# Seven products instead of eight for w_down, interleaved with w_up, in a one-core decoder layer

## What is computed

```
h = RMSNorm(x);  [b, c, xt, v] = h @ W_in
x = x + concat(short_conv(b, c, xt), pool_mix(v)) @ W_out
u = relu(RMSNorm(x) @ W_up)          # 2048 -> 8192
x = x + (u * u) @ W_down             # 8192 -> 2048
out = RMSNorm(x)
```

## Time and profile before

| | us |
|---|---|
| median of 3 runs | 1001.91 (1000.73 to 1002.18) |
| the profiled execution, device time | 1000.99 |
| its span in the trace | 999.2 |
| TensorE busy in it | 986.5 |
| VectorE busy | 586.4 |
| ScalarE busy | 419.6 |
| GpSimd busy | 1.4 |

### The profile page before, as it was taken

The page is one execution under the profiler, slowest core; times in us unless marked ns, Lnnn a source line. Parts: engine busy times, 40 slices in busy tenths (PEclk is TensorE's granted clock), DMA queues, the critical chain, the costliest instruction groups (busy, mean ns, idle before and its releaser), DMA issues.

```text
span 999.2 us, 12457 instructions
## 1 busy us (share of the span) xinstructions
PE 986.5 (99%) x5088; PEld 847.2 (85%) x5088; DVE 586.4 (59%) x428; ACT 419.6 (42%) x325; POOL 1.4 (0%) x9
## 2 busy tenths in 40 slices
PE   8999999999999999999999999999999999999996
PEld 7888888888888888888888888888888888888885
DVE  6597777655554766544656654556565445656453
ACT  6644435354443434333444433343433334444342
POOL 0000000000000000000000000000000000000000
PEclk9999999999999999999999999999999999999998
DMA  9956543555544655555455455545545554555512
GB/s 327 392 194 229 190 188 122 215 211 190 189 169 169 233 189 195 183 208 177 165 211 206 176 203 191 187 151 213 209 183 207 176 204 132 211 209 205 187 66 84
DMA packets 29694, 193.52 MB, mean 194 GB/s; under 512 B 3296, under 2 KB 3552, under 8 KB 7136
## 3 DMA queue, kind: packets, MB, share of 16 engines
q1 hardware_dynamic: 29232, 190.85, 52.1%
q10 hardware_dynamic: 288, 1.18, 0.3%
q0 software_dynamic: 144, 1.05, 0.3%
HBM read 190.97 MB, written 2.10 MB: 193 GB/s over the span
## 4 chain that ended last, share of the span: by engine, by line
PE 94%; DMA 3%; SPq 1%; DVE 1%; ACT 0%; issue 0%; ACTq 0%
PE ps L343 44%; PE ps L252 33%; PE ps L255 17%; DMA w_raw<-w_stream 3%; SPq L208 1%; PE ps L277 0%; PE ps L329 0%; SPq L193 0%; DVE w_lo L628 0%; ACT w_hi L449 0%; PE ps L317 0%; DVE val L635 0%; PE ps L276 0%; PE ps L279 0%; ACT cross L483 0%
## 5 line engine op out<-in xcount | busy, mean ns | idle before, releaser
L628 DVE TENSOR_TENSOR w_lo<-w_raw,w_hi 128x2048 fp32r<-128x2048 f32 x172 | 392.0, 2291 | 280.4 <-ACT w_hi L449 279.7
L449 ACT ACTIVATE w_hi<-w_raw 128x2048 fp32r<-128x2048 f32 x172 | 326.8, 1912 | 344.0 <-PE ps L343 210.8
L252 PE MATMUL ps<-act_a,w_hi 128*128 128x512 f32 x1472 | 351.1, 391 | 0.0
L343 PE MATMUL ps<-w_hi,act_b 128*128 128x512 f32 x1280 | 345.3, 390 | 0.0
L252 PEld LDWEIGHTS ps<-act_a,w_hi 128*128 128x128 f32 x1472 | 271.0, 188 | 52.5
L343 PEld LDWEIGHTS ps<-w_hi,act_b 128*128 128x128 f32 x1280 | 239.8, 188 | 49.3
L343 PE MATMUL ps<-w_lo,act_b 128*128 128x512 f32 x640 | 199.7, 389 | 0.0
L255 PEld LDWEIGHTS ps<-act_a,w_lo 128*128 128x128 f32 x1472 | 188.6, 191 | 7.0
L255 PE MATMUL ps<-act_a,w_lo 128*128 128x256 f32 x1472 | 191.1, 283 | 0.0
L343 PEld LDWEIGHTS ps<-w_lo,act_b 128*128 128x128 f32 x640 | 120.2, 188 | 25.0
L635 DVE TENSOR_TENSOR val<-ps,cross 128x1024 f32<-128x1024 f32 x26 | 31.8, 1223 | 47.2 <-ACT cross L455 47.2
(11 more groups left out here) (68 smaller groups left out, 164.3 us busy)
## 6 DMA issues: line engine op xcount, KB each, us to landing
w_raw<-w_stream SPq DMA_DIRECT2D x172, 1024.0 KB, 4.8
w_raw<-w_stream SPq DMA_DIRECT2D x16, 256.0 KB, 7.9
x<-x_rows SPq DMA_DIRECT2D x2, 1024.0 KB, 17.4
mix_mem<-x_t SPq DMA_DIRECT2D x3, 512.0 KB, 8.2
out<-x SPq DMA_DIRECT2D x6, 256.0 KB, 2.7
mix_mem<-pool_w ACTq DMA_DIRECT2D x1, 1024.0 KB, 9.1
mix_mem<-g_final POOLq DMA_DIRECT2D x1, 1024.0 KB, 5.0
out<-val SPq DMA_DIRECT2D x2, 256.0 KB, 2.1
```

Source lines behind the costliest of these rows:

```text
L252: return pe.matmul(ps[:, bank, :], weights_hi, act, start=first, stop=False)
L343: mm = pe.matmul(ps[:, NT * parity + t, :], a[:, at:at + P], cols, start=first and i == 0, stop=last and i == 2)
L449: act.activation(w_hi[:, c, :], w_raw[:, c, :], ACT.Copy).then_inc(hi_ready, 1)
L628: dve.tensor_tensor(out=w_lo[:, c, :], in0=w_raw[:, c, :], in1=w_hi[:, c, :].bitcast(F32), op=ALU.subtract)\
```

## The change

The `w_down` product is cut into units. A unit takes 1024 rows of `w_down` (the output of two `w_up` blocks, one even, one odd) and 1024 of its columns, as a 2 x 2 grid of quadrants of 512 x 512: B11, B12 (one half of the rows), B21, B22. The activations are a 2 x 2 grid too: 128 tokens by 512 features each, A11 to A22. A11 and A12 are the first 128 tokens, A11 and A21 the features of the even block. The plain way needs eight products of quadrants, this one seven, of sums of quadrants; each product is 12 matmuls of 512 columns (`term`). Fourteen of the sixteen units are done so, the last two (`plain`) the old way, in eight chunks of 24 matmuls.

The seven terms of unit d and the weights that they take:

| term | activations | weights |
|---|---|---|
| A11_B11 | A11 | B11 |
| S5_T1 | S5 = A22 - A21 | T1 = B12 + B11 |
| N3_B22 | N3 = -N6 - A12 | B22 |
| N6_T2 | N6 = -A11 - S5 | T2 = T1 + B22 |
| S7_T3 | S7 = A11 - A21 | T3 = B22 + B12 |
| A12_B21 | A12 | B21 |
| A22_T4 | A22 | T4 = T2 + B21 |

(The signs sit in the sums of activations and in the additions onto `x`.) T1 is a GpSimd `tensor_tensor` of 128 x 2048 floats, the rest of the sums are DMAs that add onto what lies in SBUF (`accum_op=ALU.add`), issued by GpSimd. One step handles the `w_up` block t = d + 2 and the unit d. Its eleven items are numbered, each takes one of four slots of `w_hi` and `w_lo`: U0, A11_B11, S5_T1, U1, N3_B22, N6_T2, U2, S7_T3, U3, A12_B21, A22_T4, where U0 to U3 are the chunks of `w_up`.

```
+A11_B11, S5_T1, N3_B22, N6_T2, S7_T3, A12_B21, A22_T4 = 1, 2, 4, 5, 7, 9, 10
+STEPS = 11
...
@@ sync
+            for t in range(LEAD, UPS):
...
+                load_quad(w_raw[:, 2, :], d, 0, up_item(1, 2) if lead else term_item(d - 1, A12_B21),
+                          raw_loaded[2])
+                load_up(t, 2, up_item(t, 0))
+                sp.wait_ge(t1_added, d + 1)
+                load_quad(w_raw[:, 2, :], d, 2, term_item(d, A11_B11), raw_loaded[2])
+                load_up(t, 3, up_item(t, 1))
...
@@ gpsimd
-            pool.wait_ge(value_ready, 2)
+            def add_quad(to, d, n, after, added):
+                pool.wait_ge(lo_ready, after + 1)
+                pool.dma_start(to, w_quads[4 * d + n, :, :], accum_op=ALU.add).then_inc(added, 16)
+            def add_to_base(d):
+                pool.wait_ge(raw_loaded[2], 16 * (FIRST_UP + LEAD + 2 * d + 1))
+                pool.wait_ge(sum_base_loaded[d % 2], 16 * (d // 2 + 1))
+                pool.tensor_tensor(out=sums[d % 2], in0=sums[d % 2], in1=w_raw[:, 2, :], op=ALU.add)\
+                    .then_inc(t1_added, 1)
+            for d in range(SEVENS):
+                add_to_base(d)
+                add_quad(sums[d % 2], d, 3, term_item(d, S5_T1), t2_added)
+                add_quad(w_raw[:, 3, :], d, 1, term_item(d, N3_B22), t3_added)
+                add_quad(sums[d % 2], d, 2, term_item(d, N6_T2), t4_added)
...
@@ tensor
+            for t in range(LEAD, UPS):
+                d = t - LEAD
+                up_chunk(t, 0)
...
+                    pe.wait_ge(folded, FOLDS * d)
+                term(d, A11_B11, A11, NT, True)
+                term(d, S5_T1, S5, NT + 1, True)
+                up_chunk(t, 1)
+                pe.wait_ge(folded, FOLDS * d + 2)
+                term(d, N3_B22, N3, NT + 1, False)
+                term(d, N6_T2, N6, NT, False)
+                up_chunk(t, 2)
+                pe.wait_ge(folded, FOLDS * d + 4)
+                term(d, S7_T3, S7, NT, False)
+                up_chunk(t, 3)
+                term(d, A12_B21, A12, NT + 2, True)
+                pe.wait_ge(folded, FOLDS * d + 5)
+                term(d, A22_T4, A22, NT, False)
...
@@ scalar
+            def hi_of(g, raw):
+                act.wait_ge(chunk_used, g - 3)
+                act.activation(w_hi[:, g % 4, :], raw, ACT.Copy).then_inc(hi_ready, 1)
...
+                act.wait_ge(t2_added, 16 * (d + 1))
+                hi_of(term_item(d, N6_T2), sums[d % 2])
...
@@ vector
+                up_lo(t, 0)
+                add_up(t - 1)
+                lo_of(term_item(d, A11_B11), w_raw[:, 2, :])
...
+                    fold(d - 1, 6, A12_B21, NT + 2, 0, 0, ALU.add)
+                dve.wait_ge(t1_added, d + 1)
+                lo_of(term_item(d, S5_T1), sums[d % 2])
...
+                fold(d, 1, A11_B11, NT, 0, 0, ALU.add)
+                lo_of(term_item(d, N6_T2), sums[d % 2])
...
+                fold(d, 2, S5_T1, NT + 1, 1, 1, ALU.subtract)
+                up_lo(t, 2)
+                lo_of(term_item(d, S7_T3), w_raw[:, 3, :])
+                fold(d, 3, N3_B22, NT + 1, 0, 1, ALU.subtract)
+                up_lo(t, 3)
+                fold(d, 4, N6_T2, NT, 0, 1, ALU.subtract)
+                lo_of(term_item(d, A12_B21), w_raw[:, 2, :])
+                lo_of(term_item(d, A22_T4), sums[d % 2])
```

More of the change, by code:

```diff
@@ L404, in _ @@
             pe.wait_ge(inv_rms_ready, 2)
[L405 to L422, removed]
@@ L440, in _ @@
+            plain(5, range(HALVES), True)
+            for t in range(HALVES):
+                plain(6, (t,), False)
+                plain(7, (t,), False).then_inc(half_done, 1)
         @block.scalar
@@ L581, in _ @@
             root(1, 0, HALVES)
[L583 to L597, removed]
@@ new lines, in up_hi, with take_up @@
+            def up_hi(t, c):
+                loads = FIRST_UP + LEAD + 2 * (t - LEAD) + c // 2 + 1
+                act.wait_ge(raw_loaded[c % 2], 16 * loads)
+                hi_of(up_item(t, c), w_raw[:, c % 2, :])
+            def take_up(t):
+                act.wait_ge(chunk_used, up_item(t, CHUNKS - 1) + 1)
+                if t >= 3:
+                    act.wait_ge(quad_ready, quad_count((t - 3) // 2, N3))
+                act.wait_ge(summed, turn(FIRST_UP) + t)
+                banks = bank_halves(1 if t == 1 else 0, 1)
+                act.activation(cross[:, :, :], banks, ACT.Copy).then_inc(cross_ready, 1)
@@ new lines, in plain_hi @@
+            def plain_hi(f):
+                slot, loads = plain_raw(f)
+                act.wait_ge(raw_loaded[slot], 16 * (loads + 1))
+                hi_of(FIRST_PLAIN + f, w_raw[:, slot, :])
+            plain_hi(0)
+            take_up(UPS - 1)
+            plain_hi(1)
+            square_up(UPS - 1)
+            act.wait_ge(squared, UPS)
+            quad_hi(SLICES - 1, A12, val[:, :, 0:P], A12_B21)
+            quad_hi(SLICES - 1, A22, val[:, :, P:S], A22_T4)
+            for f in range(2, PLAINS):
+                plain_hi(f)
@@ new lines, in plain_lo, with add_rows_of @@
+            def plain_lo(f):
+                lo_of(FIRST_PLAIN + f, w_raw[:, plain_raw(f)[0], :])
+            def add_rows_of(j, f, bank):
+                dve.wait_ge(chunk_used, FIRST_PLAIN + f + 1)
+                dve.tensor_tensor(out=x_cols(j), in0=ps[:, bank:bank + HALVES, :], in1=x_cols(j),
+                                  op=ALU.add).then_inc(rows_added, 1)
+            last_slice = SLICES - 1
+            fold(SEVENS - 1, 5, S7_T3, NT, 1, 1, ALU.subtract)
+            quad_lo(last_slice, A21, held[:, :, P:S])
@@ new lines, in _ @@
+            plain_lo(0)
+            add_up(UPS - 1)
+            plain_lo(1)
+            fold(SEVENS - 1, 6, A12_B21, NT + 2, 0, 0, ALU.add)
+            dve.wait_ge(squared, UPS)
+            quad_lo(last_slice, A12, val[:, :, 0:P])
+            quad_lo(last_slice, A22, val[:, :, P:S])
+            plain_lo(2)
+            fold(SEVENS - 1, 7, A22_T4, NT, 1, 0, ALU.add)
+            plain_lo(3)
+            plain_lo(4)
+            plain_lo(5)
+            dve.wait_ge(folded, FOLDS * SEVENS)
```

339 lines of the change are left out of this document (283 added, 56 removed).

## The result

The changed kernel takes 1052.83 us (median of 4 runs, 1048.23 to 1054.76), the kernel before 1001.32 (4 runs, 1000.36 to 1002.18): 1.0508 times as long, interval 1.0468 to 1.0548. The forecast was 1020 us. The profiled execution has a span of 1052.7 us, 53.5 over the one before. The seven products are done in 168 fewer matmuls, and the kernel is slower by 5%.

A forecast was written before the change was run, and what follows sets the result against it. TensorE's matmuls bound the kernel before; afterwards a dependency loop through an adding DMA: 34.9 + 9.4 + 1.0 = 45.3 us a step, 1.26 over 44.04. Fourteen steps +17.6, join 1.3, from 1000.99: 1020 us, range 1000 to 1038 (8 in 10: 972 to 1065).

The forecast's parts named there:

- its loop: From U3's end through DVE's tail and splits, T2's adding DMA, fold and N3_B22 to the next U3's end: 34.9 + L.
- the collision: GpSimd's sum for T1 running beside DVE's work: takes 1.0 us a step from DVE, between 0 and 4.6.
- L: Time from issue to landing of T2's adding DMA: 5.0 + 2.86 for a second stream + 1.5, 9.4 us.
- the join: Last step to first plain chunk: fold 6 behind the w_up tail and a split on DVE, a stall of 1.3 us.
- the 38.1 us of the matmuls: TensorE in the fourteen units: 168 fewer matmuls at 0.227 us; a step's matmuls take 41.3 us against 44.04.
- The clock: All TensorE matmuls were priced at 0.227 us; a lower clock was listed only under "wrong altogether".
- The 1.5 for loads alongside: Addition to T2's landing time for two SP loads sharing the DMA engines: 1.5 us, about half of one load.
- Rival 3: GpSimd's sum and DVE exclude each other for the whole sum: 3.6 us more a step, 48.9, 1070 us; chance 0.10.
- more idle time in folding steps: TensorE idles 1.4 us more in folding steps, where DVE has one more sum and lo part, than in others.
- idle time in front of A11_B11: TensorE waiting before a unit's first term: listed as a sign that another chain leads, forecast wrong altogether; no size given.
- rival 2: Adding DMAs queue behind each other and the loads, L 11 to 14, T3's loop binds too: 1056 us; chance 0.22.
- Rival 1: The adding DMA is quick, L 5 to 7.5, TensorE stays the bound: 964 to 993 us, middle 975; chance 0.26.

The follow-up runs named there:

- filler run: The changed kernel plus 118 matmuls into an unused bank, in front of TensorE's waits before A11_B11 or N3_B22 in alternate steps: 1044.54 us, ratio 1.0427.
- folds 6 and 7 early: Against a 1016.07 us kernel (reordered, sum on DVE, join wait cut): on DVE add_up ahead of the sum, the last two folds right behind it; 1011.46 us.
- the own bank: The changed kernel with N3_B22 in an unused bank, without its wait for fold 2, which covers both halves of x in one instruction: 1052.20 us, ratio 1.0526.
- the order mended and no adding: The reordered 1011.46 us kernel (sum on DVE) with its three adding loads a step made plain, sums T2 to T4 left out: 972.66 us, ratio 0.9721.

## Why the prediction was wrong

It had the sign and the chain; the size was off, 51.5 us slower by the medians and 19 forecast. The term that failed by the most is the last leg of its loop, "3 x 2.72 + 2 x 5.57 = 19.3": every matmul at full rate behind the wait. The legs of the loop, in the mean of the thirteen steps behind the first, read from the timelines:

| leg | forecast, us | measured, us |
|---|---|---|
| U3's end to the issue of T2's DMA, with the collision and the handoffs | 10.7 | 11.2 |
| T2's landing, L | 9.4 | 8.8 |
| landing to the start of N3_B22 | 5.9 | 6.0 |
| N3_B22 to the end of U3 | 19.3 | 20.7 |
| together | 45.3 | 46.7 |

The step is 1.4 us longer than forecast, 20 us in fourteen. The wait at the join is 8.9 us over its 1.3, and the first step 3.6 over the others. That is 32 of the 34.6 us between 53.5 and the 18.9 of the sum; where the last 2 lie is open. By the prediction's own steps:

- **What bounds the kernel before, and the 38.1 us of the matmuls:** right. A step without the adding takes 41.56 us.
- **The clock:** the step that failed. The prediction costed every matmul at 0.227 us whatever stood in front of it, and had a lower clock only among the things that would prove it wrong. The last leg took 1.4 us more than its 19.3: 0.8 are matmuls at half rate, 0.3 waits in front of S7_T3, the rest restarts. Over whole steps 17 us went into half rate, but a part of that falls outside the loop and is hidden in the next wait. The waits read in the timeline (2.56 us at 683.04, 1.98 at 623.31) are followed by matmuls at half rate. The exact share of the clock in the 53.5 can't be told from that of the waits, since the two feed each other: a slow term pushes U3 back and with it the next loop. The filler run got 8.3 us back on top of 27 us of useless work.
- **The loop and L:** the loop is there, with the instructions and waits foretold. L was put at 9.4 and is 8.8 for T2; the 10.5 in the table is T2's median with T4's, which lands later. The doubled time of the engines was right (5.3 us for 1 MB against 2.75). The 1.5 for loads alongside was 0.9, in the direction of a shorter step.
- **The collision of the sum with DVE:** mis-sized. The length was right, 4.62 us against 4.6. What it takes from DVE was put at 1.0 a step; it is 1.7, since the sum started 2 to 3 us later than forecast. Moving the sum to DVE gained 14.6 us. Rival 3 had the mechanism, the lock, but as a whole sum each step, which did not come.
- **The order of the steps:** "more idle time in folding steps" is wrong for this chain. In front of N3_B22 TensorE waited 10.3 us in the folding steps and 22.0 in the others. The folding steps have the longer list, but T2 lands a good 1 us later in the others; why is open.
- **A11_B11:** "idle time in front of A11_B11" was named as what would prove the forecast altogether wrong. It is there, 15.2 of 50.9 us, 12.6 of them in the folding steps: fold 7 stands on DVE behind two splits and the quadrants. The prediction followed one chain and did not ask what the banks of the next step wait for. Whether it leads in some steps is open: with folds 6 and 7 early 4.6 us came back, and the next wait came up in its place.
- **The join:** mis-sized, 1.3 us forecast, 10.2 of wait and 10.9 of time measured. The prediction costed DVE's list and overlooked ACT's, where a wait for A22_T4 stands ahead of the copy of `cross`. A needless wait of one quadrant, in a line that runs once.
- **The rivals:** rival 2 (1056 us) is nearest by number, and half of it is there. T3 and T4 land in 11.3 and 12.1 us, as it said, and T3's chain binds as T2's does: freed of the one, TensorE waited as long for the other (the own bank). But T2, on which its step of 47.9 us is built, lands in 8.8 and not in 12, so it comes near the measured time by luck, without the clock and with 1.3 us for the join. Rival 1 is refuted by the landings.

As a sum over the runs: 28 us faster with the order mended and no adding (972.66). Adding takes 39 of it back (1011.46). The order of DVE's list, the join and the sum on GpSimd, each with its share of the low clock, take the other 41 (1052.83). The last three are not independent, and no split of the 41 into exact shares is claimed: the join is 11, the sum 15, and some 15 are the rest.

## What to carry to other kernels

When a bound engine gets less work but more waits, price the wait and what follows it: read the clock in the stretch, and add a share of the work behind the waits at half rate. Here that was 17 us beside 52 us of waits, behind 11 of 26 of them. A DMA in a dependency loop is priced by its time to landing, and the loop's slack is the number to find first; here it was 41.3 - 34.9 = 6.4 us, and the adding DMA took 8.8 where the plain one took 5.2. Where a schedule's chains are all about equally long, removing one wait shows nothing, so test such edits together and measure the step, not the wait. And read every engine's list at a join: one wait for the wrong product cost 11 us, a fifth of the 53.5.

## What the runs showed of the hardware

- An accumulating DMA into SBUF took the DMA engines 5.3 us for 1 MB, a plain one 2.75 to 2.9. It landed after medians of 8.7 (T2), 11.3 (T3) and 12.1 us (T4), where the plain one in its place took 5.1, 7.1 and 6.9. GpSimd spent 0.87 us on its issue against 0.53 to 0.57.
- A GpSimd `tensor_tensor` over two SBUF operands (128x2048, 4.62 us where it came first) and DVE's SCALAR_TENSOR_TENSOR excluded each other: 1.22 us became up to 4.17. While the first pass over the block, which reads `ps`, ran beside it (657.80, 1.22 us), neither lost anything.
- 118 useless matmuls in front of waits made the kernel faster by 8.3 us, with the granted clock over the steps at 0.99 in place of 0.96.
